# Hybrid RG-LRU / RWKV-7 / PEER layer on one core: projection and query tiles with a 512-column operand, the RG-LRU chain moved up, the first V rows loaded in 24 parts

## What is computed

```
h = rms_norm(x) ;  p = h @ w_in                  # 2048 -> 5408 columns, 43 tiles of 128 when padded
A: xc = causal_conv4(p_xb) + b
   a = exp(-8 sigmoid(xc @ wa) softplus(-lam)) ; bx = sqrt(1 - a^2) * sigmoid(xc @ wi) * xc
   y_lru = scan(h_t = a_t h_{t-1} + bx_t) * gelu(p_gate)
B: RWKV-7 on shifted columns (p + (prev - p) * mu): 16 heads of 64, delta-rule state scan,
   group norm, bonus, gate -> y_rwkv
x = x + concat(y_lru, y_rwkv) @ w_out
PEER: q = rms_norm(x) @ wq ; 2 x top 16 of 128 keys per head and token, best 16 pairs,
      softmax ; sum of gelu(h . u_e) * gate * v_e over the chosen experts
out = rms_norm(x + peer)
```

## Time and profile before

| | before |
|---|---|
| median of 3 runs | 1985.81 us (1983.82 to 1986.44) |
| the profiled execution, its own time | 1986.91 us |
| its span in the profile | 1985.1 us |
| granted PE clock, mean | 0.995 of full |
| busy: PE, PEld, DVE, ACT, POOL | 97%, 87%, 77%, 49%, 25% |
| HBM read / written | 434.44 MB / 29.43 MB |
| chain that ended last | PE 87%, DVE 5%, DMA 3%, ACT 3% |

### The profile page before, as it was taken

The page is one execution under the profiler, slowest core; times in us unless marked ns, Lnnn a source line. Parts: engine busy times, 40 slices in busy tenths (PEclk is TensorE's granted clock), DMA queues, the critical chain, the costliest instruction groups (busy, mean ns, idle before and its releaser), DMA issues.

```text
span 1985.1 us, 36029 instructions
## 1 busy us (share of the span) xinstructions
PE 1930.5 (97%) x14368; PEld 1733.2 (87%) x14368; DVE 1523.4 (77%) x2339; ACT 970.6 (49%) x1394; POOL 501.0 (25%) x511
## 2 busy tenths in 40 slices
PE   7999999999999999999999999999999999999997
PEld 7999898887899888888888888888988888888886
DVE  5557575667534999987878888757888999999998
ACT  5535343555544444444444444445674444444444
POOL 0000000000000000000012222204667667677673
PEclk9999999999999999999999999999999999999999
DMA  7524233245655656565678888867979999999996
GB/s 239 182 87 128 87 118 97 66 152 177 203 179 169 184 189 185 187 185 186 189 227 282 287 285 286 277 189 233 307 235 363 365 369 368 363 385 377 377 374 256
DMA packets 149607, 466.25 MB, mean 235 GB/s; under 512 B 19936, under 2 KB 45056, under 8 KB 148928
## 3 DMA queue, kind: packets, MB, share of 16 engines
q1 hardware_dynamic: 115760, 335.36, 51.4%
q0 software_dynamic: 33680, 128.58, 17.7%
HBM read 434.44 MB, written 29.43 MB: 234 GB/s over the span
## 4 chain that ended last, share of the span: by engine, by line
PE 87%; DVE 5%; DMA 3%; ACT 3%; issue 1%; DVEq 0%; SPq 0%; ACTq 0%
PE ps L1719 87%; DMA oneJ<-oneJ_spill 2%; DVE lo L1081 1%; ACT hi L678 1%; DMA raw<-in_w_in 1%; DMA raw<-in_w_out 0%; DVE hT L1089 0%; DVE xc L1089 0%; DVE TmTT L1293 0%; DVE L L1276 0%; DVE lr L1388 0%; PE ps L1879 0%; ACT x_sq L893 0%; DMA x_sb<-in_x 0%; DMA raw<-in_wq 0%
## 5 line engine op out<-in xcount | busy, mean ns | idle before, releaser
L1719 PE MATMUL ps<-hT,hi 128*128 128x512 f32 (+1 forms) x3936 | 1076.8, 346 | 9.9 <-DVE rkv L1089 4.7
L1719 PE MATMUL ps<-hT,lo 128*128 128x256 f32 x2992 | 840.5, 281 | 0.0
L1719 PEld LDWEIGHTS ps<-hT,hi 128*128 128x128 f32 x3936 | 682.2, 191 | 109.4 <-DVE rkv L1089 5.5
L1081 DVE TENSOR_TENSOR lo<-raw,hi 128x1024 fp32r<-128x1024 f32 x406 | 492.3, 1224 | 227.4 <-ACT hi L678 220.9
L678 ACT ACTIVATE hi<-raw 128x1024 fp32r<-128x1024 f32 x406 | 424.4, 1060 | 443.6 <-DMA raw<-in_peer_u 372.0
L1719 PEld LDWEIGHTS ps<-hT,lo 128*128 128x128 f32 x2992 | 569.2, 190 | 0.0
L636 POOL DMA_INDIRECT got<-in_peer_v,row_ids x256 | 329.6, 1287 | 140.4 <-DVE sums L1089 106.7
L955 ACT ACTIVATE vhi<-vraw 128x960 fp32r<-128x960 f32 (+1 forms) x256 | 197.7, 791 | 257.0 <-DMA vraw<-in_peer_v 239.7
L1579 DVE TENSOR_TENSOR vlo<-vraw,vhi 128x960 fp32r<-128x960 f32 (+1 forms) x256 | 227.4, 889 | 30.8 <-ACT vhi L955 22.0
L1719 PE MATMUL ps<-vhi,a_hi 128*128 128x480 f32 (+1 forms) x768 | 245.3, 374 | 1.6 <-DVE a_lo L1635 1.6
L1719 PE MATMUL ps<-vhi,a_lo 128*128 128x480 f32 (+1 forms) x768 | 245.4, 374 | 0.0
(11 more groups left out here) (288 smaller groups left out, 1790.3 us busy)
## 6 DMA issues: line engine op xcount, KB each, us to landing
raw<-in_peer_u SPq DMA_DIRECT2D x256, 512.0 KB, 4.3
vraw<-in_peer_v SPq DMA_DIRECT2D x128, 480.0 KB
raw<-in_w_in SPq DMA_DIRECT2D x86, 512.0 KB, 3.5
vraw<-in_peer_v SPq DMA_DIRECT2D x128, 224.0 KB
raw<-in_w_out SPq DMA_DIRECT2D x32, 512.0 KB, 3.6
raw<-in_wq SPq DMA_DIRECT2D x32, 512.0 KB, 3.5
oneJ_spill<-madeJ POOLq DMA_DIRECT2D x64, 256.0 KB, 5.1
oneJ<-oneJ_spill SPq DMA_DIRECT2D x64, 256.0 KB, 4.8
```

The lines of the kernel that those rows point to most:

```text
L1081: V.tensor_tensor(lo[n % NR][:, :], raw[n % NR][:, :], hi[n % NR][:, :].bitcast(F32), ALU.subtract).then_inc(lo_done, 1)
L1719: return nc.tensor.matmul(o, lhsT, rhs, start=start, stop=stop, skip_group_check=True)
```

## The change

Four edits.

- **Tiles of w_in and wq.** `project` and `tile_part` now issue what `wide_tile` did (which goes away): a 512-column matmul and a 256-column one in place of three with 256 columns. The bank then holds two halves. A new DVE step, `add_halves(t)`, adds them with a reduction over the two halves, writes `zt` (two buffers in SBUF, or `xpad` for xb tiles) and frees the bank. `result` reads `zt` on both engines. `add_halves(t-1)` stands ahead of `los(t)`. For the query tiles ACT copies the lower half and a new DVE step `q_add` adds the upper one and frees the bank.
- **RG-LRU.** The first four channel tiles' gate products stand ahead of the last group's "yt" on PE, the next four behind the first piece of w_out. ACT and DVE begin the chain ahead of the last `yR_hi` and `yR_lo`; `lr`, `li`, `la`, `lt` get places of their own.
- **w_out** pieces go in another order (`OUT_ORDER`: four first halves, four second halves, then as before).
- **V.** The first eight loads (480 or 224 KB) become 24 of up to 256 columns (128 KB), from step 5 on every second step, in place of step 10 and every sixth.

```diff
-V_FIRST, V_EVERY = 10, 6
+V_PART = 256
+V_EARLY = [(k, first, min(first + V_PART, end)) for k in range(2 * V_RAWS)
+           for start, end in [(V_PIECE * (k % 2), V_PIECE * (k % 2) + N_V_COLS[k % 2])]
+           for first in range(start, end, V_PART)]
+V_FIRST, V_EVERY = 5, 2
...
+            def load_v_early(n):
+
+                k, first, end = V_EARLY[n]
+                sync.dma_start(vraw[k // 2][:, first:end], a["peer_v"][k // 2, :, first:end]).then_inc(
+                    sem(f"v_in{k}"), 16)
...
+            def add_halves(t):
+
+                wait_full(dve, "tile", t)
+                if RESULTS[max(t - 1, 0)]:
+                    dve.wait_ge(sem("result_in"), RESULTS[t - 1])
+                z = xpad[:, 3:3 + SEQ] if ORDER[t][0] == "xb" else zt[t % 2][:, :]
+                V.tensor_reduce(z, bank("tile", t).rearrange("p (a t) -> p t a", a=2), AX_X,
+                                ALU.add).then_inc(freed("tile", t), 1)
...
             def tile(t):
 
+                if t:
+                    add_halves(t - 1)
                 los(t)
...
+            def q_add(t):
+
+                dve.wait_ge(sem("z_in"), t + 1)
+                V.tensor_tensor(qT[t % 2][:, :], bank("tile", T_Q + t)[:, SEQ:2 * SEQ], qT[t % 2][:, :],
+                                ALU.add).then_inc(freed("tile", T_Q + t), 1)
...
-                    mm(o, wh, hT_hi[:, kc], half == 0 and k == 0, False)
-                    mm(o, wh, hT_lo[:, kc], False, False)
-                    ins = mm(o, wl, hT_hi[:, kc], False, half == 1 and k == 7)
+                    mm(o.rearrange("p (a t) -> p a t", a=2), wh, hT[:, :, kc], half == 0 and k == 0,
+                       False)
+                    ins = mm(o[:, 0:SEQ], wl, hT_hi[:, kc], False, half == 1 and k == 7)
...
+                if g == GROUPS - 1:
+                    pe.wait_ge(sem("wai_in"), 32)
+                    for c in LRU_HALF[0]:
+                        lru_gates(c)
                 o = job("yt")
```

More of the change, by code:

```diff
@@ L104 @@
 PICKS = HEADS * TOPK
+RESULTS = [sum(kind != "xb" for kind, _ in ORDER[:t]) for t in range(N_IN + 1)]
 SHIFTED = [t for t, (kind, _) in enumerate(ORDER) if kind in ("lora", "r", "k", "v")]
 MU = {t: {"r": 0, "k": CT, "v": 2 * CT, "lora": 3 * CT}[ORDER[t][0]] + ORDER[t][1] for t in SHIFTED}
+OUT_ORDER = [(c, half) for half in range(2) for c in range(4)] + [
+    (c, half) for c in range(4, N_OUT) for half in range(2)]
 MARKS = [range(9, 18), range(18, 27), range(27, 36), range(36, N_IN)]
@@ L251, in hybrid_layer_kernel @@
         lora = nx("lora", [P, 3, SEQ])
+        zt = [ar(f"zt{i}", 31000 + SEQ * i, [P, SEQ]) for i in range(2)]
         group_at = f[0]
@@ L481, in _ @@
                 load(n, a["w_in"][n // 2, n % 2])
-            for c in range(N_OUT):
+            for n, (c, half) in enumerate(OUT_ORDER):
                 ch = (c + CT) % KC
-                for half in range(2):
-                    load(2 * (T_OUT + c) + half,
-                         a["w_out"][ch * P:(ch + 1) * P, half * PIECE:(half + 1) * PIECE])
+                load(2 * T_OUT + n, a["w_out"][ch * P:(ch + 1) * P, half * PIECE:(half + 1) * PIECE])
             for t in range(N_Q):
@@ L845, in _ @@
                                              bias=gneps_c).then_inc(sem("gsd_done"), 1)
[L846 to L851, removed]
+                if g < GROUPS - 1:
+                    act.wait_ge(sem("y_f32"), g + 1)
+                    nc.scalar.activation(yR_hi[:, 2 * g:2 * g + 2, :], yT[:, :, :], ACT.Copy).then_inc(
+                        sem("yR_hi"), 1)
+                assert not marks or g == GROUPS - 1
+            result(N_IN - 1)
             def hi_out(first, last):
@@ L856, in hi_out, with lru_in, lru_decay @@
                     hi_piece(2 * T_OUT + n)
[L858 to L867, removed]
+            def lru_in(h):
+                for c in LRU_HALF[h]:
+                    wait_full(act, "lru", c)
+                    nc.scalar.activation(lr[:, c], bank("lru", c)[:, 0:SEQ], ACT.Tanh, scale=0.5,
+                                         bias=hba[:, c:c + 1])
+                    nc.scalar.activation(li[:, c], bank("lru", c)[:, SEQ:2 * SEQ], ACT.Tanh, scale=0.5,
+                                         bias=hbi[:, c:c + 1]).then_inc(freed("lru", c), 1)
+            def lru_decay(h):
                 for c in LRU_HALF[h]:
@@ L1741, in tile_part @@
                     pe.wait_ge(lo_done, n + 1)
-                o = bank("tile", t)[:, 0:SEQ]
+                o = bank("tile", t)
                 for k in range(first, last):
@@ L1813, in _, with lru_gates @@
             pe.wait_ge(sem("lora_done"), 1)
+            def lru_gates(c):
+                pe.wait_ge(sem("conv_done"), c + 1)
+                wait_free(pe, "lru", c)
+                for q in range(2):
+                    ins = mm(bank("lru", c)[:, q * SEQ:(q + 1) * SEQ], wai[:, q, c], xc[:, c],
+                             q == 0, q == 1)
+                ins.then_inc(full[PLAN["lru", c][0]], 1)
             for g in range(GROUPS):
```

171 lines of the change are left out of this document (88 added, 83 removed).

## The result

| | before | after, first series | after, once more (own series) |
|---|---|---|---|
| median | 1984.72 us of 5 runs (1980.44 to 1986.44) | 1967.89 us of 5 (1966.55 to 1974.39) | 1977.06 us of 5 (1973.19 to 1977.83) |
| ratio to before, 95% interval | | 0.9925 [0.9908, 0.9942] | 0.9955 [0.9942, 0.9969] |
| profiled execution, span | 1985.1 us | 1966.1 us | 1973.1 us |

What follows compares the result with a forecast made beforehand. PE, busy 97% of the span, was taken as the bound; terms -6.0 - 2.9 + 1.1 - 4.9 + 0.5 (queries) - 4.0 gave -16.2 us against 1986.91, stated as 1970 us, range 1962 to 1979.

Steps and rivals of the forecast that it cites:

- Pace of the tiles: PE's w_in and query tiles: each 0.155 us shorter where PE sets the end, 38.5 tiles, -6.0 us.
- Banks at the first tiles: First tiles on PE: bank waits of 1.4 (lora) and 1.52 us go, since add_halves frees the bank earlier, -2.9 us.
- ten tiles of pace: Share of the pace term for the 10 tiles up to the first group's first part, at 0.155 us each.
- First parts: First parts of the four groups: DVE's reductions against its idle time; `L` 0.3 us earlier in groups 1 and 2, sum +1.1 us.
- The waits named for groups 1 and 2: PE in groups 1 and 2: no bank wait left, but lo waits of one to two us ahead of `m(3)`.
- The slow clock "behind them": Groups 1 and 2: the low clock behind PE's bank waits of 1.36 and 1.7 us is swallowed with them.
- one sign named as wrong: Chunk loops: PE waits ahead of the use of `SA` would show the forecast wrong.
- RG-LRU: RG-LRU stage: PE's waits for convolution (1.4) and ACT (1.2) go, lo waits of 2.8 shrink to 0.5, -4.9 us.
- V's parts: Picking stage: V's loads in 128 KB parts remove two thirds of PE's 6.4 us of `oneJ` waits, -4.0 us.
- Rival 1: V's parts in 1 KB lines cost DMA time, PE waits 1.4 us more, total 1975 us; chance 0.17.
- The U tiles: U tiles, already in the new form: no change forecast, 0 us.

Runs made afterwards that it cites:

- the old form in the first parts: Version with x in eight parts, the 12 tiles of m(0) to m(3) in groups 0 to 2 put back to three 256-column matmuls without reduction: 1972.13 us, ratio 0.9932.
- x in eight parts: Kernel after, the 2 MB load of x for the second norm cut into eight of 256 KB, each released by a later w_out piece: 1969.97 us, ratio 0.9925.
- old RG-LRU with x in eight: Kernel after, RG-LRU edit and w_out order undone, load of x for the second norm in eight parts: 1978.62 us, ratio 0.9954.
- the version with other banks: Version with x in eight parts and last key scores behind the first U tile, U tile i taking the bank tile i+2 had: 1963.45 us, ratio 0.9892.

## Why the prediction was right, and where it was not

**Pace of the tiles (-6.0).** A query tile with its scores takes 6.00 us (6.19 before), blocks of 0.3467; of the tiles of w_in most run at 0.3533 and some at 0.3467. So the two values that I averaged are both there. The query stage gave -2.44, with a wait of 0.58 ahead of the last score, against -2.0. Here the Trainium skill's rule (TensorE: Matmul & The Clock Gate, "Wait — 56ns, not 53.3ns?") would have had 2.5 ns a block, and the rows have 6.7 or 13.3: the trace does not agree.

**Banks at the first tiles (-2.9), with ten tiles of pace (-1.55).** -3.99 and -5.13 against -4.45: right.

**First parts (+1.1).** 691 ns for a reduction was taken exactly. Groups 1 and 2 came within 0.8 us, group 3 at +2.16 and +1.68 for +1.2; its wait for lo is 2.98 us, 0.6 more than before where I had 1.3. The run with twice the reductions agrees with the sum but can't confirm the terms, since the clock took part; the old form in the first parts shows that reductions and bank waits trade about one for one. The waits named for groups 1 and 2 are there: none for a bank, and 1.26 and 2.15 us for lo (at 182.02 and 271.79). The slow clock "behind them" went in group 1 alone (178 to 182 us: 0.61 before, 1.00 after); in group 2 the first profile after still has 0.58 from 272 to 276, where the second is at full clock and 0.7 us faster. And one sign named as wrong did show, in two of 16 places: 1.3 us more ahead of the use of `SA`. The forecast had DVE's idle time there as enough.

**RG-LRU (-4.9): the term that failed.** "DVE has its chain begun when the lo pieces of w_out are wanted" was right for DVE and left out the load of x. The waits named (`li`, convolution) went, and with x in eight parts the edit is worth 4.8 us (163.02 to 158.19), as forecast. In the kernel as changed it is worth nothing, because the 2 MB load that waits for the same `yR_lo` now meets w_out pieces that PE wants: one takes 9.71 us to land, and PE waits 3.9 us for lo behind the last group, where the forecast had left 0.5. I had costed the moves on PE, ACT, DVE and not on POOL's queue. That `yR_lo` itself moves was in the diff (`low_rows` behind the chain's first steps).

**V's parts (-4.0).** By the ratio of that edit alone, -4.8. What follows the U tiles took 3.5 to 6.4 us less than in the first profile before in eleven of the twelve profiles with the parts, and 1.2 less in the twelfth (old RG-LRU with x in eight), the one with 3.4 us of waits for `oneJ`; the two profiles of before differ by 2.4 themselves. Rival 1 is out.

**The U tiles (0).** They gave -6.92 in the first profile and nothing in the second. The forecast took each half's pace as fixed, although had the same code at both. That the first series landed near 1970 was luck: this gain, unforeseen, and V's extra 1.2 stood in for the RG-LRU's 4. With the U tiles alike the change is worth 12 us by either pair of profiles (19.0 - 6.9, and 12.0), and 9 by the medians of the second series, not 16. Both series lie in the range.

## What to carry to other kernels

When an edit brings a semaphore forward or back, list every queue that waits for it, the DMA queues first: a big load that rode in the shadow of a stall meets the pieces that PE now wants. Cut such a load into parts and release each by the progress of the stage; together the two gave the 4.8 us back here, and which of them did is not shown. And compare stages, not only totals, where a long stream of like matmuls can run at two paces: half a stage at the other pace is worth as much here as the rest of an edit.

## What the runs showed of the hardware that I had not expected

A block of a 512-column and a 256-column matmul, each with its weight load, runs at 0.3467 or 0.3533 us with the granted clock at 1.00 in both, and keeps its pace over a thousand blocks. In the U tiles it changed only at breaks in the stream: in the ten profiles with wide query tiles and the wait for `q_add` at the start of the U tiles, 8 went from 0.3467 to 0.3533 there and 2 stayed; at the six transposes `idx`, all ten profiles that had been slow became fast, three stayed fast, and one became slow (356.16 us for the second half). The four key-score matmuls, without a wait, left every fast stream fast and made all eight slow ones that met them fast (six behind the second query tile, one behind the third, one behind the first U tile). The four transposes put into the U tiles kept the pace six times out of eight. And a break is not always needed: between the first and the second query tile, where no other instruction stands, the pace changed in five of the eleven profiles with wide query tiles (in the version with other banks from 0.3533 to 0.3467, without a wait). What decides at a break is open; what is shown is that one program takes either, and that without the wait the last version kept the faster one in its profile.
